# Input x, turned, in four parts on ScalarE's DMA queue, and six products of zeros ahead of the first tile

## The reference

```python
h = rms_norm(x, norm1_g[l])      # x * rsqrt(mean(x*x) + eps) * g
z = h @ w_in[l]                  # one combined projection
z_a, u_raw, v_raw, gate_logits = jnp.split(z, [COLS_A, COLS_A + WIDTH_B, COLS_A + 2 * WIDTH_B], axis=-1)
```

## Time and profile before

| | |
|---|---|
| median of three runs | 1233.29 us |
| time of the profiled execution | 1235.86 us |
| its span, first to last instruction | 1234.0 us |
| PE busy | 1192.6 us, 97% |
| DMA in slices 11 to 39 of 40 | 9 tenths or more |
| mean granted clock of PE | 0.991 |

### The profile page before, as it was taken

One profiled execution on the slowest core, in us unless ns is written; L12 is line 12 of the kernel. 1 busy time (PEld: TensorE's weight loads), 2 busy tenths in 40 slices (PEclk: granted clock), 3 DMA queues, 4 the chain that ended last, 5 costly groups with the idle time before them and its releaser, 6 DMA issues.

```text
span 1234.0 us, 16299 instructions
## 1 busy us (share of the span) xinstructions
PE 1192.6 (97%) x7270; PEld 570.3 (46%) x7270; DVE 295.9 (24%) x658; ACT 188.6 (15%) x361; POOL 8.3 (1%) x19
## 2 busy tenths in 40 slices
PE   9999999999999999999999999999998989998997
PEld 6788588875433343433333333334343333333332
DVE  3175544343421112111111201112111111111111
ACT  3453213333201000001000000000000000010002
POOL 0000000000000000000000000000000000000000
PEclk9999999999999999999999999999999999999989
DMA  9341655259899999999999999999999999999994
GB/s 322 124 133 70 222 206 162 88 227 418 350 424 430 426 427 428 432 431 431 432 431 427 434 431 431 433 426 434 430 430 435 429 430 431 431 433 430 424 428 183
DMA packets 37276, 448.57 MB, mean 364 GB/s; under 512 B 11648, under 2 KB 11792, under 8 KB 18640
## 3 DMA queue, kind: packets, MB, share of 16 engines
q1 hardware_dynamic: 27072, 441.02, 85.2%
q0 software_dynamic: 1232, 3.95, 1.0%
q10 hardware_dynamic: 8896, 2.49, 0.9%
HBM read 445.35 MB, written 2.10 MB: 363 GB/s over the span
## 4 chain that ended last, share of the span: by engine, by line
PE 72%; DMA 26%; DVE 1%; issue 0%; ACT 0%; DVEq 0%; SPq 0%
PE ps L1715 27%; DMA ring<-w_gate_up 26%; PE ps L1305 8%; PE ps L1740 8%; PE ps L1399 7%; PE ps L1694 5%; PE ps L1769 4%; PE ps L1386 2%; PE ps L1591 2%; PE ps L1723 2%; PE ps L1759 1%; PE ps L1750 1%; PE ps L1336 1%; PE ps L1654 1%; DMA consts<-cst 0%; PE ps L1316 0%
## 5 line engine op out<-in xcount | busy, mean ns | idle before, releaser
L1715 PE MATMUL ps<-ring,xacc 128*64 128x512 f32 x2048 | 465.7, 601 | 19.5 <-DMA ring<-w_gate_up 19.3
L1715 PEld LDWEIGHTS ps<-ring,xacc 128*64 128x64 f32 x2048 | 142.4, 137 | 307.2 <-issue 299.7
L1740 PE MATMUL ps<-ring,aT 128*64 128x512 f32 x992 | 220.3, 596 | 8.2 <-DMA ring<-w_down 8.2
L1740 PEld LDWEIGHTS ps<-ring,aT 128*64 128x64 f32 x992 | 73.7, 138 | 149.9 <-issue 149.9
L1246 DVE TENSOR_SCALAR gc<-ps 128x512 f32<-128x512 f32 x32 | 22.1, 691 | 391.7 <-PE ps L1715 391.7
L1189 DVE TENSOR_TENSOR xacc<-ps,consts 128x512 f32<-128x512 f32 x30 | 20.7, 691 | 338.2 <-PE ps L1694 338.2
L1305 PE MATMUL ps<-hT,wbuf 128*128 128x256 f32 x384 | 87.0, 383 | 0.0
L1399 PE MATMUL ps<-hT,wbuf 128*128 128x256 f32 x384 | 85.9, 381 | 0.0
L1305 PEld LDWEIGHTS ps<-hT,wbuf 128*128 128x128 f32 x384 | 71.8, 190 | 13.9 <-issue 4.7
L1399 PEld LDWEIGHTS ps<-hT,wbuf 128*128 128x128 f32 x384 | 72.1, 190 | 11.2 <-issue 1.4
L827 ACT ACTIVATE sgm<-gc 128x512 f32<-128x512 f32 x32 | 20.2, 630 | 360.8 <-DVE gc L1246 360.7
(11 more groups left out here) (263 smaller groups left out, 705.9 us busy)
## 6 DMA issues: line engine op xcount, KB each, us to landing
ring<-w_gate_up SPq DMA_DIRECT2D x44, 4096.0 KB, 36.8
ring<-w_down SPq DMA_DIRECT2D x22, 4096.0 KB, 35.1
ring<-w_gate_up SPq DMA_DIRECT2D x38, 2048.0 KB, 16.6
ring<-w_down SPq DMA_DIRECT2D x17, 2048.0 KB, 19.1
wbuf<-w_in SPq DMA_DIRECT2D x25, 512.0 KB, 3.9
wbuf<-w_in SPq DMA_DIRECT2D x12, 1024.0 KB, 6.1
ring<-w_down SPq DMA_DIRECT2D x6, 1024.0 KB, 35.2
wbuf<-w_in SPq DMA_DIRECT2D x2, 2048.0 KB, 8.6
```

Source lines behind the costliest of these rows:

```text
L1715: last = mm(bank(GU_BANK + q, 0, 512, slice(64 * half, 64 * half + 64)), x_, w[:, :, half, :], start=k == 0, stop=k == KT - 1, skip_group_ ...
L1740: last = mm(bank(b, 0, 512, slice(64 * half, 64 * half + 64)), turned[:, c0:c0 + SLOTS], w[:, D * r + 512 * half:D * r + 512 * (half + 1)] ...
```

## The change

SP no longer issues xt. ACT issues it in four quarters of 256 KB (blocks 0 and 1, 2 and 3, 4 and 5, 6 and 7), with the head of the constants behind the first quarter. DVE waits for quarter 1 for blocks 0 and 1, for quarter 2 for blocks 2 and 3, and for both last quarters, which share a semaphore, for blocks 4 to 7. PE multiplies six products of zeros instead of four.

```diff
-        WARM = 4
+        WARM = 6
 ...
-            half = KT * T // 2
             for i in range(2):
-                sp.dma_start(xT0[:, i * half:(i + 1) * half], xt[:, i * half:(i + 1) * half]).then_inc(sm["turned_in" if i == 0 else "turned_rest_in"], 16)
                 sp.dma_start(unit(0)[:, 512 * i:512 * (i + 1)], w_in_block("a", 0)[:, 512 * i:512 * (i + 1)]).then_inc(sm["first_half"] if i == 0 else unit_sem("a", 0), 16)
 ...
-            act.dma_start(cs_[:, 0:HEAD + P], cst[:, 0:HEAD + P]).then_inc(sm["head_in"], 16)
+            quarter = KT * T // 4
+            for i in range(4):
+                if i == 1:
+                    act.dma_start(cs_[:, 0:HEAD + P], cst[:, 0:HEAD + P]).then_inc(sm["head_in"], 16)
+                cols = slice(i * quarter, (i + 1) * quarter)
+                act.dma_start(xT0[:, cols], xt[:, cols]).then_inc(sm[("turned_in", "turned_next_in", "turned_rest_in", "turned_rest_in")[i]], 16)
 ...
-                dve.wait_ge(sm["turned_rest_in" if k >= KT // 2 else "turned_in"], 16)
+                dve.wait_ge(sm[("turned_in", "turned_next_in", "turned_rest_in", "turned_rest_in")[k // 2]], 16 if k < KT // 2 else 32)
```

More of the change, by code:

```diff
@@ L279, in build @@
                  "sp_done sp_out sq_ready ss_ready stored sumsq sumsq_rest tk_done tr_done turned_in u_done u_out "
-                 "raw_ready rs_out turned_rest_in z_scaled "
+                 "raw_ready rs_out turned_next_in turned_rest_in z_scaled "
                  "ug_ready up_done up_sig upw_in v_out var_done vc_out vn_ready w1_done w1_out wo_read wr_ready ws_in wst_ready "
```

## The result

The changed kernel takes 1239.85 us in the median of five runs (1239.54 to 1240.69), against 1233.29 before. The ratio is 1.0052, with a 95% interval of 1.0041 to 1.0064: slower by 6.4 us, between 5.1 and 7.9. The profiled execution took 1240.0 us, its span is 1238.2.

What follows compares the result with a forecast made beforehand. PE's chain from the first data to `spread_roots` was taken to bound the kernel, its delay reaching the end. Later data +3.1 and clock +1.7 gave +4.8 us on the median 1233.3: 1238.1 us, range 1233.2 to 1239.8.

Steps and rivals of the forecast that it cites:

- The wait that takes the place of the one removed: First tile: queues alternate packet by packet, so xt's last quarter comes 4.5 us later than the last half did; `spread_roots` +3.1 us.
- Rival B: Queues at the start take turns by bytes, not packets: ACT's transfers done at 10.0, +0.9 us, 1234.2; chance 0.14.
- Rival A: Start: xt and head arrive ahead of SP's bytes, PE does not pause; -1.0 us, 1232.3; chance 0.09.
- When the last quarter lands: Arrivals of xt: the last quarter, paired with the second half of x, lands at 12.24 us, behind 3196 KB.
- this is one curve: Arrivals in the first 12 us: bytes landed by a given time are the same in any order, 3196 KB by 12.24.
- rival E: Clock stays down through the second tile, or small packets slow both queues at the start: 1240 or more; chance 0.06.
- From the landing to `spread_roots`: First tiles on PE: 0.65 us to pick-up, then 24 records in 5.4 us, plus 1.7 for the clock.
- Rival C: First tile: packets in turn, but PE's clock stays up; +3.1 us, 1236.4; chance 0.17.
- the term of the clock: PE behind the pause of 2.1 to 3.0 us: clock falls to its lower level, +1.7 us (bounds 0 and 5.4).
- The two more products of zeros: PE before the first tile: they end by 6.7 us, within the wait for data, and cost nothing.
- The rest: ACT's four more issues (1.7 us), SP's earlier issues and the roots (ready 15.5, below 18.3): all hidden.
- Rival D: Experts' weight stream: its slack absorbs the delay later, 1233.3 us; chance 0.02.

Runs made afterwards that it cites:

- run 4: The changed kernel with xt on ACT's queue in two halves (rows of 4096 B) instead of four quarters: 1235.35 us, ratio 1.0017.
- run 6: The changed kernel with SP waiting for all of xt before it issues the plain x: 1237.11 us, ratio 1.0025.
- run 7: The changed kernel with the plain x on SP's queue in four transfers (rows of 2048 B) instead of two (4096 B): 1238.05 us, ratio 1.0033.
- run 5: The changed kernel with eight products of zeros ahead of the first tile, two more between blocks 1 and 2, seven between 3 and 4: 1238.03 us, ratio 1.0033.
- run 1: The changed kernel with four products of zeros instead of six: 1240.3 us, ratio 1.0055.

## Why the prediction was right

*The wait that takes the place of the one removed.* Right, and it was the bulk. Quarters of xt take turns with longer rows, 303 to 303 packets; runs 4, 6 and 7 each changed one factor of that (packets of xt, presence of x, row length of x) and moved the end of xt as computed beforehand (10.48, 10.71 and 12.25, for 9.7 to 10.5, 10.5 to 11.4 and 12.0 to 12.6). Rival B (turns by bytes) had it landing at 10.0 in any cut: 13.55 refutes it, and so do run 4, in which xt landed 3.1 us earlier with the same bytes, and run 7. Two rows of 2048 B to a turn would have given two packets of q10 for each of q1; they were equal in number. Rival A (ACT's queue is served ahead) likewise.

*When the last quarter lands.* The mechanism was right, the term mis-sized: "this is one curve, whatever the order, that many bytes have landed by that time" gave 12.24, it was 13.55. The head was late already, 7.6 instead of 6.58, quarter 2 at 9.7 instead of 8.42. A small part is the start-up, the second half of rival E: up to 4 us the queues moved about as many packets as before (175 against 191), but 0.36 MB instead of 0.51. Windows after, then before, with GB/s as the last number:

```profile
2.00:4.50 2.50, 2.50 (x7) 1.00 0.82 172
4.50:7.00 2.50, 2.17 (x6) 1.00 0.97 359
```

```profile
2.00:4.50 2.50, 2.50 (x7) 1.00 0.83 239
4.50:7.00 2.50, 0.89 (x3) 1.00 0.98 330
```

By 7 us that is 1.33 MB against 1.42 MB, 0.2 us of the later rate.

The rest is not a lower rate, but bytes that went to transfers further back. The five pairs hold 3196 KB, 3.27 MB. When the second half of x landed before, at 12.24, 3.63 MB had been moved in all; when the last quarter landed now, at 13.55, it was 4.03. These 0.40 MB more take 1.0 us at 410 GB/s. The queues up to 12.24 us, and from there to 13.55:

```profile
q1 hardware_dynamic: 826, 2.33, 53.3%
q10 hardware_dynamic: 710, 1.16, 30.8%
...
q1 hardware_dynamic: 165, 0.53, 102.6%
q10 hardware_dynamic: 10, 0.01, 2.7%
```

At the predicted time 710 of q10's 720 packets had been moved. The last ten took another microsecond, in which q1 had nearly all of the engines' time, and a transfer lands only with its last packet. It was the same with the head (300 packets of q10 by 6.58, where it and the first quarter hold 288) and with quarter 2 (438 by 8.42, for 432). So the curve was right for nearly all of a transfer and too early for its last packets. Why this tail is longer with two full queues is not shown; that the 16 engines then get less even is my guess.

*From the landing to `spread_roots`.* PE took up block 4 at 0.44 us after the landing, not 0.65: -0.2. The 24 records took 7.03 us, where 5.4 + 1.7 = 7.1 stood. Run 5 measured the clock's part alone: 7.03 - 5.34 = 1.7. Rival C (the clock stays up) fell with the 0.50 of the granted clock.

That the term of the clock came out at 1.7 is in part luck. The prediction let the clock fall in the long pause ("one of 2.64 brought it down"). It had fallen at about 10.4 us, behind pauses of 1.48 and 0.87 us and ahead of the one of 2.05; in run 7 it fell at about 8.8, behind a single pause of 1.91, and the same 24 records took 6.91 us. In run 1 they took 7.99. So the wait for the last quarter was not needed for the fall, and the size of the term changes from trace to trace, between 1.6 and 2.7 us over the 5.34 of run 5.

*The two more products of zeros* I had priced at nothing, "since PE waits for data". Nothing shows that they cost anything. The reason was too short, as what PE does ahead of a wait can change when the clock comes back behind it; but the 0.9 us by which run 1 was later at `spread_roots` is no more than what the clock does from one execution to the next (4.46 to 5.49 us for the same twelve records), so no value for them is shown.

*The rest* was hidden as said: ACT's table load went from 1.20 to 3.50 us with only one activation of 0.20 us behind it until 11.49, and the roots were ready 4.3 us before PE. Rival D (absorbed by the stream's slack) fell: SP's gate moved by 6.25 us.

*Sum.* Predicted +4.8 (+3.1 and +1.7), measured +5.8 at `spread_roots` and +6.4 (5.1 to 7.9) in the run times. The gap of 1.0 at `spread_roots` is 1.3 for the landing, -0.2 for the pick-up and -0.1 for the 24 records. Of the other 0.6, 0.4 is the second fall of the clock near 320 us in the one trace; all of it lies inside the interval. The median, 1239.85, stands at the very edge of the range, which ended at 1239.8, and outside the 1237.0 to 1239.5 of the forecast alone: the mechanism was right, and the landing was priced too low.

## What to carry to other kernels

A second queue did not add bandwidth here (396 to 421 GB/s with two full queues, 412 to 418 with one); it changed who waits. As long as critical transfers stand first on one queue they are ahead of everything behind them, while on a queue of their own they get one packet for each packet of the other queue, and the shorter rows get the fewer bytes. So before moving a load, pair the transfers of both queues by their packet counts and add up the bytes ahead of it, and allow for the last packets: here they made up about 1 us of each landing. And where an unavoidable wait splits PE's work into short pieces, count the clock: the work behind it may run at half pace for some microseconds (7.03 us instead of 5.34 here), and products of zeros in the gap can buy that back, as in run 5.

## What the runs showed of the hardware

Turns between queues did not look at size: 303 to 303 packets, nearly all of 4096 and 2048 B. A transfer can be late by its last packets alone: 710 of 720 were moved by 12.24 us, the rest by 13.3. A load on one queue can be sped up by shortening the rows of another queue (13.58 to 12.25).

The granted clock fell behind pauses shorter than the 2.64 us of the earlier trace rows, and the same pauses do not always bring it down. In run 7 it fell at about 8.8 us, behind one pause of 1.91; in the changed kernel at about 10.4, behind pauses of 1.48 and 0.87. Single pauses of 1.73 in run 4 and among the experts and of 1.83 in run 5 left it up. Near 320 us it fell in three of nine traces, behind pauses of 0.37, 0.27 and 0.57 us that were as long in the other six. And the first microseconds of a trace can read 1.00 where the pace is that of the lower level: the eight records of four products of zeros took 3.78 us, and in run 5, with the clock up, 24 records of the same size took 5.34.
